# Five projections and the output product of a transformer block as three products of rounded parts, with one ring slot given to the high parts

## The reference

```python
mod = jax.nn.silu(c) @ w_ada[l] + b_ada[l]
shift1, scale1, gate1, shift2, scale2, gate2 = jnp.split(mod, N_MOD, axis=-1)
h = modulate(rmsnorm(x, norm1_w[l]), shift1, scale1)
proj = h @ w_in[l]
r_q, r_k, r_v, r_g, d_q, d_k, d_v, d_z, d_a, d_b = jnp.split(proj, cuts, axis=-1)
ret = retention(rotary(r_q), rotary(r_k), r_v);  ret = rmsnorm(ret) * silu(r_g)
dn = gated_delta_rule(l2norm(...), l2norm(...), ...);  dn = rmsnorm(dn, dn_norm_w) * silu(d_z)
x = x + gate1 * (jnp.concatenate([ret, dn], axis=-1) @ w_out[l])
h2 = modulate(rmsnorm(x, norm2_w[l]), shift2, scale2)
x = x + gate2 * hierarchical_moe(h2, ...)      # 32 experts, 2 of them for each token
```

## Time and profile before

| | |
|---|---|
| median of 3 runs | 986.25 us (985.26 to 987.01) |
| profiled execution | 986.98 us, its span 985.1 us |
| PE busy | 919.2 us (93%) |
| DVE, ACT, POOL busy | 414.5, 236.9, 130.2 us |
| granted TensorE clock, mean | 0.986 of full speed |
| DMA | 294.97 MB, mean 299 GB/s |
| chain that ended last | PE 66%, DMA 29% |

### The profile page before, as it was taken

How to read it: one execution, slowest core, us unless ns; L and a number is a source line. 1 busy time by engine, 2 the same in 40 slices (tenths; PEclk the granted TensorE clock), 3 DMA queues, 4 the chain that set the end, 5 groups by cost and what they waited for, 6 DMA issues and landing times.

```text
span 985.1 us, 12175 instructions
## 1 busy us (share of the span) xinstructions
PE 919.2 (93%) x4957; PEld 553.1 (56%) x4957; DVE 414.5 (42%) x716; ACT 236.9 (24%) x356; POOL 130.2 (13%) x145
## 2 busy tenths in 40 slices
PE   7999999999999998989885899988989899999998
PEld 4686757664553443333332344433433799999987
DVE  2454412232444342323321233323323678888843
ACT  1125203111221111101010111101011636655532
POOL 0003454021110000000000000000000102232300
PEclk9999999999999999999997999999999999999999
DMA  9989328268699999999999999999999655665411
GB/s 342 278 188 268 112 86 277 77 245 339 243 380 404 407 407 416 398 409 404 411 413 409 379 398 403 412 412 402 422 420 394 225 173 194 196 200 180 171 43 43
DMA packets 87783, 294.97 MB, mean 299 GB/s; under 512 B 11198, under 2 KB 35254, under 8 KB 63015
## 3 DMA queue, kind: packets, MB, share of 16 engines
q1 hardware_dynamic: 82311, 286.63, 77.6%
q10 hardware_dynamic: 3008, 5.44, 1.5%
q0 software_dynamic: 2400, 2.04, 0.8%
HBM read 297.81 MB, written 2.10 MB: 304 GB/s over the span
## 4 chain that ended last, share of the span: by engine, by line
PE 66%; DMA 29%; issue 2%; DVE 1%; ACT 1%; POOL 0%; ACTq 0%; DVEq 0%
DMA ring<-in_w_dram 25%; PE ps L886 9%; PE ps L464 7%; PE ps L1006 6%; PE ps L1005 6%; PE ps L1007 6%; PE ps L453 5%; PE ps L548 4%; PE ps L909 4%; PE ps L889 4%; PE ps L726 3%; DMA arena<-in_w_dram 2%; PE ps L479 2%; PE ps L448 1%; PE ps L928 1%
## 5 line engine op out<-in xcount | busy, mean ns | idle before, releaser
L889 PE MATMUL ps<-ring,proj 128*64 128x512 f32 x288 | 129.4, 596 | 15.0 <-DMA ring<-in_w_dram 15.0
L886 PE MATMUL ps<-ring,proj 128*64 128x512 f32 x272 | 126.9, 607 | 1.8 <-issue 1.6
L889 PE MATMUL ps<-arena,proj 128*64 128x512 f32 x224 | 104.6, 616 | 10.7 <-DMA arena<-in_w_dram 10.7
L886 PE MATMUL ps<-arena,proj 128*64 128x512 f32 x240 | 110.4, 603 | 2.5 <-issue 2.3
L1486 DVE TENSOR_TENSOR proj<-RQ,ps 64x512 f32<-64x512 f32 x32 | 22.1, 690 | 211.7 <-PE ps L871 114.6
L1005 PE MATMUL ps<-h_h,w_h 128*128 128x256 f32 x336 | 95.1, 283 | 0.0
L1006 PE MATMUL ps<-h_l,w_h 128*128 128x256 f32 x336 | 95.1, 283 | 0.0
L1007 PE MATMUL ps<-h_h,w_l 128*128 128x256 f32 x336 | 95.1, 283 | 0.0
L1648 DVE TENSOR_TENSOR w_l<-ring,w_h 128x2048 fp32r<-128x2048 f32 x33 | 75.5, 2291 | 44.8 <-ACT w_h L1931 44.8
L1896 ACT CAST MX_r<-RQ 64x512 fp32r<-64x512 f32 x64 | 39.5, 617 | 196.7 <-DVE RQ L1503 196.0
L1931 ACT CAST w_h<-ring 128x2048 fp32r<-128x2048 f32 x33 | 62.7, 1902 | 83.2 <-PE ps L1007 77.0
(11 more groups left out here) (316 smaller groups left out, 1514.8 us busy)
## 6 DMA issues: line engine op xcount, KB each, us to landing
ring<-in_w_dram SPq DMA_DIRECT2D x108, 1024.0 KB, 27.0
arena<-in_w_dram SPq DMA_DIRECT2D x84, 1024.0 KB, 27.1
ring<-in_w_ada_dram SPq DMA_DIRECT2D x11, 2048.0 KB, 11.3
ring<-in_ffn_w_in_dram SPq DMA_DIRECT2D x22, 1024.0 KB, 7.7
ring<-in_w_in_dram SPq DMA_DIRECT2D x6, 2048.0 KB, 19.9
ring<-in_ffn_w_out_dram SPq DMA_DIRECT2D x5, 2048.0 KB, 8.0
arena<-in_w_in_dram SPq DMA_DIRECT2D x2, 2048.0 KB, 18.2
ring<-in_w_out_dram SPq DMA_DIRECT2D x2, 2048.0 KB, 10.1
```

Of the source, the lines that this page charges most:

```text
L886: pe.matmul(ps[0:SLOTS, :], XTe[i % 2][:, k, :], u1[:, k, :], start=(k == 0), stop=(k == 7))
L889: t = pe.matmul(ps[64:64 + SLOTS, :], XTe[i % 2][:, k, :], u3[:, k, :], start=(k == 0), stop=(k == 7))
```

## The change

The eight-chunk float32 product of a segment becomes two parts of four chunks, `project(s)` with s from 0 to 9, and each part three sets of matmuls: rows high by weights high, rows high by weights low, rows low by weights high (`four_chunks`). The output product is parted in the same way (s from 10 to 13). ACT writes a part's high half into slot 3 of the ring, half a slot in turn (`higher(s)`), and DVE puts the low half where the weights were (`lower(s)`). The rows' high parts are made by ACT and lie in `vrow` and `gates[:, 1]`, the low ones by POOL in `hT` (for the output product by DVE, `mixed_low`). Slot 3 is no longer in the ring in stage 1, so all units go through slots 0 to 2. Segment 2 moves behind `bt` and `at`. Ada 9 moves ahead of segment 4, ada 10 behind it, ada 11 behind the first half of the output product (both stood behind the router's logits). Rotations of q and k move one level later. The bias of the last modulation vector is loaded later, on ACT's queue.

```diff
@@ slots, parts
-        for i, name in enumerate([("ada", 0), ("ada", 1), ("ada", 2), ("ada", 3), ("dn", 2), ("proj", 2), ("proj", 0),
-                                  ("proj", 1), ("ada", 4), ("ada", 5), ("ada", 6), ("proj", 3), ("ada", 7), ("ada", 8),
-                                  ("proj", 4), ("ada", 9), ("wo", 0), ("wo", 1), ("ada", 10), ("ada", 11)]):
-            units.place(name, i % R)
+        HIGH = 3
+        for name, s in ((("ada", 0), 0), (("ada", 1), 1), (("ada", 2), 2), (("ada", 3), HIGH), (("dn", 1), R + 1), (("dn", 0), R),
+                        (("dn", 2), 0), (("proj", 2), 1), (("proj", 0), 2), (("proj", 1), 0), (("ada", 4), 1), (("ada", 5), 2),
+                        (("ada", 6), 0), (("proj", 3), 1), (("ada", 7), 2), (("ada", 8), 0), (("proj", 4), 1), (("ada", 9), 2),
+                        (("ada", 10), 0), (("wo", 0), 2), (("ada", 11), 0), (("wo", 1), 1)):
+            units.place(name, s)
+        parts = [(kind, i, half) for kind, i in (("proj", 2), ("proj", 0), ("proj", 1), ("proj", 3), ("proj", 4))
+                 for half in range(2)] + [("wo", j, half) for half in range(2) for j in range(2)]
@@ PE
-            def by_token(name, ps, w, n):
-                for k in range(8):
-                    i = pe.matmul(ps[:, 0:512], hT[:, k, tok(n)], w[:, k, 0:512], start=(k == 0), stop=(k == 7))
-                i.then_inc(*mm.up(*name))
+            def four_chunks(ps, s, n, kind, first=False, final=False):
+                half = parts[s][2]
+                _, high, low = part_views(s)
+                w = (low if kind == 1 else high).rearrange("p (k c) -> p k c", k=4)
+                for k in range(4):
+                    rows_k = hTr[:, 4 * half + k, tok(n)] if kind == 2 else row_high[half][:, k, tok(n)]
+                    i = pe.matmul(ps[:, 0:512], rows_k, w[:, k, :], start=(first and k == 0), stop=(final and k == 3))
+                return i
...
+                pe.wait_ge(split_high, s + 1)
+                for n in range(2):
+                    four_chunks(projected[seg][n], s, n, 0, first=(half == 0))
+                pe.wait_ge(split_low, s + 1)
...
             def w_out(n, j, g):
+                s = parts.index(("wo", j, g))
+                pe.wait_ge(mixed_high, 2 * g + n + 1)
+                pe.wait_ge(split_high, s + 1)
+                four_chunks(wo[n, j], s, n, 0, first=(g == 0))
+                pe.wait_ge(split_low, s + 1)
+                four_chunks(wo[n, j], s, n, 1)
                 pe.wait_ge(*drained("m_turned", n, g))
+                i = four_chunks(wo[n, j], s, n, 2, final=(g == 1))
@@ DVE
+            def lower(s):
+                src, high, low = part_views(s)
+                ve.wait_ge(split_high, s + 1)
+                ve.tensor_tensor(low, src, high.bitcast(F32), ALU.subtract).then_inc(split_low, 1)
@@ ACT
+            def higher(s):
+                kind, i, _ = parts[s]
+                src, high, _ = part_views(s)
+                ac.wait_ge(*filled((kind, i)))
+                if s > 1:
+                    ac.wait_ge(*mm.of("part", s - 2))
+                ac.copy(high, src).then_inc(split_high, 1)
...
+            higher(11)
+            higher(12)
+            ada(11)
+            higher(13)
             turn_mixed(0, 1)
             turn_mixed(1, 1)
@@ POOL, ahead of the decay's masks
+            po.wait_ge(*mm.of("dn", 2, 3))
+            for g in range(2):
+                po.wait_ge(rows_high, g + 1)
+                po.tensor_tensor(hTr[:, 4 * g:4 * g + 4, :], hT[:, 4 * g:4 * g + 4, :], row_high[g].bitcast(F32),
+                                 ALU.subtract).then_inc(rows_low, 1)
@@ SP
-            for j in range(2):
-                load(("wo", j), w_out[:, :, 512 * j:512 * j + 512])
             load_ada(10)
+            load(("wo", 0), w_out[:, :, 0:512])
             load_ada(11)
+            load(("wo", 1), w_out[:, :, 512:1024])
```

More of the change, by code:

```diff
@@ L720, in w_out @@
             def w_out(n, j, g):
-                w = unit(("wo", j), 512)
-                if n == 0 and g == 0:
-                    pe.wait_ge(*filled(("wo", j)))
+                s = parts.index(("wo", j, g))
[4 more added lines that the diff above has]
+                four_chunks(wo[n, j], s, n, 1)
                 pe.wait_ge(*drained("m_turned", n, g))
-                for k in range(4 * g, 4 * g + 4):
-                    i = pe.matmul(wo[n, j][:, :], hT[:, k, tok(n)], w[:, k, :], start=(k == 0), stop=(k == 7))
+                i = four_chunks(wo[n, j], s, n, 2, final=(g == 1))
                 if g:
                     i.then_inc(*mm.up("wo", n, j))
+                elif n:
+                    i.then_inc(*mm.up("part", s))
             turn_mixed(0, 0)
@@ L1223, in vector_program @@
                     queries(1)
-                elif level == 3:
-                    gate_total(4)
+                elif level == 2:
+                    lower(4)
                 for n in range(2):
@@ L1258, in vector_program, with mixed_low @@
             ve.tensor_tensor(OR[1], OR[1], v4(ps), ALU.add).then_inc(*free("o1"))
+            def mixed_low(n, g):
+                ps = full("m_turned", n, g)
+                ve.wait_ge(mixed_high, 2 * g + n + 1)
+                ve.tensor_tensor(hTr[:, 4 * g:4 * g + 4, tok(n)], ps[:, :].rearrange("p (c t) -> p c t", c=4),
+                                 row_high[g][:, :, tok(n)].bitcast(F32), ALU.subtract).then_inc(*free("m_turned", n, g))
+            lower(10)
+            mixed_low(0, 0)
+            mixed_low(1, 0)
+            lower(11)
             for n in range(2):
@@ L1815, in scalar_program @@
                     turn_rotated(0)
+                    higher(6)
                     turn_rotated(1)
                     ada(6)
+                elif level == 5:
+                    higher(7)
                 elif level == 6:
@@ L1823, in turn_mixed @@
                 ps = full("m_turned", n, g)
-                ac.copy(hT[:, 4 * g:4 * g + 4, tok(n)], ps[:, :].rearrange("p (c t) -> p c t", c=4)).then_inc(
-                    *free("m_turned", n, g))
+                ac.copy(row_high[g][:, :, tok(n)], ps[:, :].rearrange("p (c t) -> p c t", c=4)).then_inc(mixed_high, 1)
             retained(0)
+            higher(8)
             retained(1)
+            higher(9)
             ada(8)
+            ada(9)
+            higher(10)
             project(4, 0)
             project(4, 1)
-            ada(9)
+            ada(10)
             ac.wait_ge(ret_rows, 2)
```

153 lines of the change are left out of this document (106 added, 47 removed).

## The result

The changed kernel takes 996.12 us (median of 8 runs, 990.04 to 997.02), the kernel before 986.66 in the same comparison. The ratio is 1.0089, 95% interval 1.007 to 1.0108: about 9 us slower, above the range on record (979.5 to 991.5). The profiled execution took 996.51 us, its span 994.7; before it was 986.98 and 985.1. So the two profiles differ by 9.6 us, about as much as the medians. Executions of one kernel lie up to 7 us apart here (with wo 1 loaded sooner, six took 983.07 to 984.92 us and six 986.82 to 989.95), so a single profile can be several us off its kernel's median.

The account below looks back on a forecast made before the run. Stage 2 was taken as bound by the hole-free stream of expert weights: start 14.9 us sooner, bytes 14.2 us more, net -0.7. That gave 986.3 us profiled, 985.5 as median (0.73 below); range 979.5 to 991.5.

Parts of the forecast that it names:

- It holds if the stream finds no hole: Expert loads, stage 2: seven slots and small loads last until 287.9, PE returns the first slot some 4 us before.
- the sum of the start (14.9) and the bytes (14.2): Expert stream, stage 2: starts 14.9 us sooner at 242.7, carries 5.77 MB more, 14.2 us; net -0.7 us.
- The step on taking turns: Ahead of the levels: POOL and DVE alternate when DVE reads two SBUF operands; transposes start at 105.6, 1.2 us later.
- the 2.7 counted for wait and clock: At the levels: PE 2.7 us late, 1.2 from waiting for POOL and 1.5 from the low clock.
- 1.5 was taken: Behind the wait ahead of the levels: low clock costs PE 1.5 us, bounds 0 and 3.
- With one or two us to spare: Around segment 4: masks, rotations and splits done in time; ada 9's unit loaded at 190.7, needed at 203.4.
- 14.3 had been taken, 7.7 was the lower bound: Load of wo 1 behind ada 11: issued at 219.2, lands 14.3 us later at 233.5; 7.7 if alone.
- Ada 10 and 11 leave the stretch of the router ... nothing: Router's stretch: 3.8 us of PE leave, filling products take their place while PE waits for DVE; effect nothing.
- The clock stays low in the output product: Rival, chance 0.26: output product at 1.2 GHz, 8 us more, first slot at 291.5, hole of 3.7 us; 990 us.
- the rival of half the rate: Segments' products: no one-pass rate, a segment 21.8 us, change 50 us slower; excluded by rows, no chance of its own.
- POOL and DVE don't take turns: Rival, chance 0.26, at the levels: masks end at 93.6, levels start at 102.5, 4.6 us less; 980.9 us.
- The products' rate: PE's segments: one-pass products 0.227 us apart, a segment 10.88 us in place of 13.73, 2.85 us less.

Follow-up runs that it names:

- the head-sum run: The changed kernel with DVE's last two head sums and their products ahead of lower(11) in place of behind it: 994.37 us, ratio 1.0072.
- the filler run: The changed kernel with additional useless filling products on PE in its longest waits of stage 1, router's stretch included: 993.23 us, ratio 1.0064.
- ada 9 behind: The changed kernel with ada 9 behind the first part of segment 4 in place of ahead of it: 989.36 us, ratio 1.0017.
- the fastest one: Changed kernel with wo 1 before ada 11, masks on DVE, ada 9 after project(8), lower(11) between head sum 3 and its scaling, router fillers: 975.88 us.

## Why the prediction was wrong

**The step that failed** is the condition under the sum: "It holds if the stream finds no hole", with the first slot back "at 283.84 - 0.3, some 4 us before that". It came back at 297.34, and the stream stood still from 293.5. Then the sum of the start (14.9) and the bytes (14.2) says nothing any more; the head-sum run shows it. The right sum from the same numbers is: the slot 13.5 us later than before, less the 3.9 us by which the stream bounds the kernel before (701.3 less 697.4), makes 9.6, the difference of the two spans. This sum is made after the fact, from the same profiles; what supports it is that the distance from the slot to the end (697.4 here) held in ten more kernels.

The 13.8 us between 283.5 and 297.34 come from PE's path, piece by piece:

- 2.2 us: the opening, which isn't the change's: it is long or short in either kernel. The second modulation unit starts at 17.98 in the profile of before and at 20.20 in that of after.
- 1.0: the levels' transposes at 108.77, of that 2.2 the opening's, against 105.6. The step on taking turns had the right place, and for this kernel the right size. The run with the masks on DVE gets 7.3 us back, more than the 2.7 counted for wait and clock, since the saving of segment 2 comes back too.
- 1.7: from there to segment 3's end. A part of a segment takes 5.63 us (121.56 to 127.19), not 5.44, so a segment saves 2.47 and not 2.85; that is 1.1 of it. The rest is the low clock, 2.3 us (3.78 against 2.38 on the transposes, 2.32 against 1.47 on what follows them, x12), where 1.5 was taken.
- 2.9: ada 9 ahead of segment 4. "With one or two us to spare" was wrong: PE waited 2.23 us for the load, then worked at the low clock. The prediction left 12.7 us from the issue of the load (190.7) to its need (203.4) and put no landing time against them. PE was ready 11.5 us after the issue (195.61 to 207.1), and the unit landed 13.6 us after it, right behind proj 4's (the first row; the second holds ada 9 and, behind it, ada 10):

```profile
193.72 0.55 SPq L2303 DMA_DIRECT2D ring<-in_w_in_dram  x1
195.61 9.72 SPq L2303 DMA_DIRECT2D ring<-in_w_ada_dram  x2
```

- minus 1.0: wo 1 landed 12.8 us after its issue and 13.2 after ada 11's (14.3 had been taken, 7.7 was the lower bound). This term was near, and the run with wo 1 ahead of ada 11 gets the wait back.
- 2.2: from the landing to wo(1, 0)'s end, at a clock of 0.54 to 0.60.
- 4.9: from there to the slot. "Ada 10 and 11 leave the stretch of the router ... nothing" stands for the largest miss: PE had these two units where it otherwise waits for DVE. Without them the clock falls to 0.50 there, the second logits take 3.60 us in place of 1.95 and the fillers behind them 6.45 in place of 4.56 (twenty at full clock, in the filler run). Fillers in three places gave 3.3 back in one kernel. That the low clock is worth this much is shown; that it is low because these two units left is argued. In the kernel before, the same move cost 1.6 us, and no run puts them back into the changed one. The output product's shorter sets are a rival: PE waits 1.13 us for DVE ahead of the first logits, and didn't before.

Counted across these pieces, PE at the low clock is some 9 us: 2.3 at the levels, 1.5 on ada 9, 2.1 behind wo 1 (2.04, 2.08 and 1.45 us for sets that take 1.1 to 1.2) and 3.3 in the router's stretch. The last is shown by an experiment of its own. The first two went away together with their waits (the masks on DVE, ada 9 behind), so there only wait and clock together are shown; the third is read from rows.

**The rivals.** "The clock stays low in the output product" was the right rival in kind and side, and the point from which it said that PE's delay decides (4.4 us) was about right: the forecast's span, 985.1 less 0.7, less the 697.3 behind the slot puts it at 287.1, 3.6 us behind 283.5 (an estimate). Its place was wrong for the larger part. It foresaw 8 us there, the rows show 2.1, and it left out the other places, so it ended 5 to 6 us short at 990 (by its own terms, 986.25 and 4.5, it is 990.8). In the rival of half the rate, seven segments' worth at 8.1 us more each would be 56 us, not 50; the rows exclude it all the same. "POOL and DVE don't take turns", by which neither would be held up, is refuted by the 8.91 us of the masks. What the prediction cites from the Trainium skill on contention (GPSIMD Engine Reference, 1. Specifications) agrees with this trace, with 4.45 us for an instruction of 2.5. The Trainium skill (SBUF — State Buffer, Who interferes with whom) goes further and calls the port pair that the two engines share an exclusive lock; 8.91 us beside an unslowed DVE agrees with that. The Trainium skill's 215.7 ns for a matmul (TensorE: Matmul & The Clock Gate, "Wait — 56ns, not 53.3ns?") is further from the measured 0.235 us of a product of a segment (5.63 us by 24) than the row that was taken, 0.227.

**What was right.** The products' rate to 4%, wo 1's late landing, the low clock behind the wait ahead of the levels (0.50). In kind, with the size somewhat off: PE's wait for wo 1 (6.39 us, 8 to 9 forecast), the wait ahead of the levels (5.67, 4 to 5 forecast).

## What to carry to other kernels

When a stream of loads is said to bound a stage, two events bound it: when it starts with how many bytes, and when the consumer gives back the first slot. Write down both times and the distance between them, and follow every small delay to the second one too; here six small ones of 1 to 5 us added up to 14 where 4 were spare. A load behind another's slot release is as late as that release, so putting two loads in the right order was worth 6 us by the profiles and 10 by the medians, at no cost. And work that is moved out of a wait may have kept the clock up there (1.6 us in the kernel before): look at what PE does in that wait afterwards.

## What was not expected of the hardware

The opening. PE's first eight filling products (x16), the same instructions in each kernel, in the changed kernel and in the fastest one:

```profile
9.70 6.36 PE L472 MATMUL ps<-consts 128*128 128x256 f32 x16 [0.88 <-DVE S L1142]
```

```profile
9.38 3.72 PE L472 MATMUL ps<-consts 128*128 128x256 f32 x16 [0.87 <-DVE S L1144]
```

Over fourteen profiles they took 3.72 us six times and 5.47 to 6.41 eight times: whatever the kernel, PE works at the higher rate from the start in some executions and only later in others. The granted clock in the profile doesn't show it: it is 1.00 from 8 to 16 us also where they took 6.36 us, so the cause stays open. The rest of stage 1 follows, up to 2.2 us later. It can account for part of the spread between executions of one kernel; where the rest of the 7 us in some of them comes from stayed open.

POOL under DVE: an instruction of 1.25 us took 7.67 us beside four instructions of DVE in a row (6.75 us in all), and DVE lost nothing. In the changed kernel it was the other way round too: a product of 128x8 elements on DVE took 2.37 us (0.17 with the rows' parts on DVE), until POOL's was done.
